# A triangular inverse built by levels: small products as 32x32 blocks on four sub-arrays, in place of 64x64 products

## The chip, the cores and the metric

The kernel runs on one core of a Trainium2 chip. The metric is the device time of one execution in microseconds. A core has a matrix engine (TensorE, PE in the tables; its weight loads are listed apart as PEld), a vector engine (DVE), a scalar engine (ACT), a third elementwise engine (POOL) and queues for transfers, which SyncE (SP) fills. Each works through its own list of instructions in order and waits for the others by semaphores. Matrix products are written to PSUM, eight banks of 512 f32 values on each of 128 partitions; everything else is held in SBUF, also 128 partitions.

## What is computed

A trunk of two layers over 528 positions of 1024 features (16 learned ones, then 512 of the input). Each layer is a half-step SwiGLU FFN, a token mixer, and another half-step FFN, with RMSNorm before and after each. The first layer's mixer is RWKV-7 time mixing, the second's is windowed attention. The change lies in the recurrence of the first mixer alone, with 16 heads of 64 features:

```python
def step(S, inp):
    r_t, w_t, k_t, v_t, a_t, b_t = inp
    sa = jnp.einsum('bhij,bhj->bhi', S, a_t)
    S = S * w_t[:, :, None, :] + sa[..., None] * b_t[:, :, None, :] + v_t[..., None] * k_t[:, :, None, :]
    return S, jnp.einsum('bhij,bhj->bhi', S, r_t)
...
_, y = lax.scan(step, jnp.zeros((B, H, N, N), f32), seq)
```

## The kernel before

The recurrence isn't run token by token. The function `core` cuts the (padded) 576 positions into NRC = 9 chunks of CH = 64 tokens. Inside a chunk each `sa` depends on the earlier ones through a strictly lower triangular 64x64 matrix, so the kernel needs the inverse of a unit triangular matrix for each head and chunk. It builds it by levels: X starts as the identity plus the entries below the diagonal within pairs of tokens, and a level l joins blocks of 2^(l-1) rows into blocks of twice that:

- `up(l, n)`: U = N_l times X, where N_l is the chunk's matrix masked to level l (levels 2 to 5; POOL makes these, L1933).
- ACT copies U from PSUM to SBUF (`copy_u`, L1783; level 6: L1786).
- `across(l, n)`: T = U times X again, in the turned form XT.
- DVE adds T to XT (`grow`, L1872) and transposes it into X by blocks of 32x32 (L1874). Level 6 only adds (L1879).

After level 5, X consists of two 32x32 blocks on the diagonal of each head's 64x64; for levels 2 to 5 all that is outside of these two blocks is zero in N_l, X, U and T. Level 6 fills the remaining corner, by `corner` (L1649 for U6, L1646 for T6), which already uses 32x32 products. Chunk 0 has no levels 5 and 6 (its first 48 positions are padding).

Layout: a pair of heads lies on the 128 partitions, one on 0 to 63 and one on 64 to 127, and there are eight pairs. Each step is done in two halves, f = 0 and 1, of four pairs. `product` (L1634) makes one matmul of 64x64 for each pair and head, so 8 for a half; operands are f32. A half of U or T lies in one PSUM bank: banks 0 and 1 hold U, 2 and 3 hold T, in the lower 256 of 512 values; `bank` gives this view.

PE's order is written out by hand in `pe`, as a software pipeline: while chunk n grows its inverse, the state products of chunk n-1 (`state_sa`, `state_s`, `state_y`), the turned operands of chunk n (`turn`, L1658: Vt, Bt, Kt) and the scores of chunk n+1 (`scores`, L1625: A, K) are put between the levels. For n at or above 1 the order is: U2 T2, SA, U3, S, T3, Y, U4, Vt Bt, A, T4, Kt, U5, K, T5, R, U6 T6. The first chunk lacks what belongs to chunk n-1 and levels 5 and 6.

Of the kernel before, what the change touches and what calls it, by code (L numbers as in the profile page):

```python
# [22 lines left out]
ALU = mybir.AluOpType  # L23
# [3 lines left out]
P = 128  # L27
# [8 lines left out]
HD = 64  # L36
# [5 lines left out]
PAIRS = HEADS // 2  # L42
# [55 lines left out]
def build(nc, xT, vecs, consts, w_gu, w_down, w_rkv, w_l1, w_g1, w_w2, w_a2, w_g2, w_out, w_q, w_k, w_v, b_v,  # L98
          w_o, rel_table, rel_hot, flip_rows, out):
    with ExitStack() as ctx:  # L100
# [15 lines left out]
        psum = ctx.enter_context(nc.psum_tensor("psum", [P, 8, 512], F32))  # L116
# [44 lines left out]
        freed = sem("banks_freed")  # L161
# [21 lines left out]
        class Plan:  # L183
# [6 lines left out]
            x = 0  # L190
# [1338 lines left out]
        def core(d_dve, c_scan, cbuf, r_end):  # L1529
# [4 lines left out]
            N = PAIRS * CH  # L1534
# [13 lines left out]
            bs = (buf(stf, 0, 2 * CH), buf(stf, 2 * N, 2 * CH))  # L1548
# [10 lines left out]
            def first(t):  # L1559
                return t[:, :, 0:CH]  # L1560
# [39 lines left out]
            def bank(n, f):  # L1600
                return psum[:, BANK[n][f], 0:N // 2].rearrange("p (q t) -> p q t", q=PAIRS // 2)

            def bank2(n, f):
                return psum[:, BANK[n][f], :].rearrange("p (q t) -> p q t", q=PAIRS // 2)

# [12 lines left out]
            def pe(e):  # L1618
# [10 lines left out]
                def product(o, f, *terms):  # L1629

                    for q in range(4):
                        for p0 in (0, HD):
                            for z, (a, b) in enumerate(terms):
                                last = e.matmul(o[p0:p0 + HD, q], a[p0:p0 + HD, 4 * f + q, 0:CH],  # L1634
                                                b[p0:p0 + HD, 4 * f + q, 0:CH],
                                                start=(z == 0), stop=(z == len(terms) - 1))
                    return last

                def corner(o, f, turned, x, xt, nt):
# [34 lines left out]
                def up(l, n):  # L1674
                    for f in range(2):
                        if l == 2:
                            after(e, i_dve, f"X{f}", n)
                        else:
                            after(e, l_dve, f"X{l - 1}_{f}", n)
                        if l < 6:  # L1680
                            after(e, i_pool, f"N{l}", n)
                            last = product(bank("U", f), f, (Nk[l], X[n % 2]))
                        else:
                            last = corner(bank("U", f), f, False, X[n % 2], XT[n % 2], first(bs[n % 2]))
                        last.then_inc(l_pe.sem, l_pe.step(f"U{l}_{f}"))

                def across(l, n):
                    for f in range(2):
                        after(e, l_act, f"U{l}_{f}", n)
                        if l == 2:  # L1690
                            after(e, l_dve, f"T6_{f}" if n > 1 else f"T4_{f}", n - 1)
                        if l < 6:
                            last = product(bank("T", f), f, (U, XT[n % 2]))
                        else:
                            last = corner(bank("T", f), f, True, X[n % 2], XT[n % 2], first(bs[n % 2]))
                        last.then_inc(l_pe.sem, l_pe.step(f"T{l}_{f}"))

                def state_r(i):
# [26 lines left out]
                        product(bank("Y", f), f, *held_state, (Vt, second(ks[i % 2])),  # L1725
                                (SA, second(bs[i % 2]))).then_inc(s_pe.sem, s_pe.step(f"Y{f}"))

                e.wait_ge(s_init, 2)
                scores_a(0)
                scores_k(0)  # L1730
                for n in range(NRC):
# [99 lines left out]
            def dve(e):  # L1831
# [32 lines left out]
                def grow(l, n):  # L1864
                    for f in range(2):
# [10 lines left out]
                        else:  # L1876
                            for p0 in (0, 64):
                                x = xt[p0:p0 + 32, :, 32:64]
                                ins = e.tensor_tensor(x, x, bank("T", f)[p0:p0 + 32, :, 32:64], ALU.add)  # L1879
                            ins.then_inc(l_dve.sem, l_dve.step(f"T{l}_{f}"))  # L1880

                def state(i):
# [9 lines left out]
                e.wait_ge(d_dve.sem, d_dve.count(f"b{KT - 1}"))  # L1892
                e.memset(ST[0][:, :, :], 0.0).then_inc(s_init, 1)
                e.memset(dec[:, :, 0:1], 1.0).then_inc(s_init, 1)
                e.wait_ge(s_init, 2)
                inverse_operands(0)
                decay_operands(0)
                masked("A", bs, 0)
# [970 lines left out]
```

## Time and profile before

| | |
|---|---|
| median of 3 runs | 2287.49 us (2283.71 to 2288.39) |
| the profiled execution | 2284.82 us |
| its span, first to last instruction | 2283.0 us |
| PE busy, share of the span | 2202.5 us, 96% |
| DVE, ACT, POOL busy | 48%, 35%, 20% |
| mean granted clock of PE | 0.975 |
| the core's stretch | 594.8 to about 818 us |

The page gives busy time by engine. The busy time of PE is a sum over modelled ends, so it can't be read as peak use. Further down the page, "the chain that ended last" goes back from the last instruction, at each step to what released it; the shares are of the span. In the rows, a line such as L1634 is a line of the kernel before. "64*64 64x64 f32" is the part of the array in use (rows*columns) and the moving operand's shape. A timeline row gives the start, the time to the end of the last record in the group, engine, line, operation, output<-inputs, the count of records, and in brackets the engine's idle time before it and what ended that. A matmul on f32 data is two records. Names are those of the SBUF areas: Nk and X, U lie in `split`, XT and one of the states in `cumsum_buf`, the masked scores in `stage`.

### The profile page before, as it was taken

To read this page: it belongs to the slowest core of one execution; us is meant where nothing else is said; L and a number is where in the kernel's file an instruction comes from. 1 tells how busy PE (TensorE), PEld (TensorE's weight loads), DVE (VectorE), ACT (ScalarE), POOL (GpSimd) and SP (SyncE) were. 2 spreads that over 40 slices of the span, in tenths; PEclk is the share of its full clock that TensorE was granted. 3 is DMA by queue.
4 is the path that set the end of the run, shared out by engine and by line. 5 is a ranking of instruction groups with operands and counts; after the bars stand their busy time and mean duration, and the time that the engine had idled before them with its cause. 6 is when DMAs were issued, how large, how long until landed. Compare 5 with 4: busy or idle time off the path is not lost.

```text
span 2283.0 us, 51042 instructions
## 1 busy us (share of the span) xinstructions
PE 2202.5 (96%) x22812; PEld 1867.3 (82%) x22812; DVE 1092.4 (48%) x1562; ACT 804.8 (35%) x1388; POOL 467.9 (20%) x595
## 2 busy tenths in 40 slices
PE   7999998999899999999999999999998999999997
PEld 6888887877699965788888888888886667888886
DVE  5433325767566555843332563333274537433323
ACT  4333313565233343533331343332142424433320
POOL 2111112420223223511110221110151204111102
PEclk9999999999999999999999999999999779999999
DMA  4323321320000012232232122232132012323311
GB/s 160 130 93 105 123 88 38 131 68 20 13 4 4 4 57 94 80 124 99 100 127 88 50 100 102 103 121 102 56 92 84 1 37 75 111 93 118 127 52 38
DMA packets 29099, 183.43 MB, mean 80 GB/s; under 512 B 3232, under 2 KB 8160, under 8 KB 9936
## 3 DMA queue, kind: packets, MB, share of 16 engines
q1 hardware_dynamic: 28032, 178.79, 22.3%
q8 instruction: 180, 2.95, 0.5%
q0 software_dynamic: 848, 1.37, 0.3%
q14 instruction: 39, 0.32, 0.0%
HBM read 174.31 MB, written 4.30 MB: 78 GB/s over the span
## 4 chain that ended last, share of the span: by engine, by line
PE 85%; DVE 10%; ACT 3%; POOL 1%; issue 1%; DMA 0%; SPq 0%; DVEq 0%; POOLq 0%; ACTq 0%
PE psum L289 67%; PE psum L1634 6%; DVE arena L355 2%; DVE arena L403 1%; PE psum L1625 1%; PE psum L381 1%; PE psum L2527 1%; PE psum L2526 1%; PE psum L2513 1%; PE psum L1658 1%; DVE arena L393 1%; DVE arena L331 1%; DVE split L264 1%; PE psum L2357 1%; DVE h L360 1%
## 5 line engine op out<-in xcount | busy, mean ns | idle before, releaser
L289 PE MATMUL psum<-x,split 128*128 128x256 f16 (+1 forms) x5568 | 638.7, 276 | 7.1 <-POOL x L422 5.5
L289 PEld LDWEIGHTS psum<-x,split 128*128 128x128 f16 x5568 | 542.9, 98 | 99.3 <-issue 15.1
L289 PE MATMUL psum<-x,split_more 128*128 128x256 f16 (+1 forms) x2496 | 287.1, 276 | 2.5 <-DVE x L2625 1.5
L289 PE MATMUL psum<-x,arena 128*128 128x256 f16 (+2 forms) x2448 | 281.1, 276 | 7.6 <-DVE arena L657 6.8
L725 POOL TENSOR_TENSOR arena<-arena 128x256 f16<-128x256 f32 (+1 forms) x176 | 120.4, 684 | 797.6 <-ACT arena L574 797.6
L289 PEld LDWEIGHTS psum<-x,split_more 128*128 128x128 f16 x2496 | 244.6, 98 | 39.6 <-issue 1.9
L289 PEld LDWEIGHTS psum<-x,arena 128*128 128x128 f16 (+1 forms) x2448 | 240.2, 98 | 43.1 <-DVE arena L264 7.3
L264 DVE SCALAR_TENSOR_TENSOR split<-stage,split 128x2048 f16<-128x2048 f32 (+1 forms) x77 | 189.9, 2467 | 157.4 <-ACT split L258 157.4
L289 PE MATMUL psum<-arena,split 128*128 128x256 f16 (+1 forms) x2304 | 261.6, 275 | 0.0
L289 PEld LDWEIGHTS psum<-arena,split 128*128 128x128 f16 x2304 | 225.4, 98 | 35.0 <-issue 2.5
L652 DVE SCALAR_TENSOR_TENSOR arena<-psum,arena 128x256 f32<-128x256 f32 (+1 forms) x176 | 75.5, 429 | 311.1 <-ACT arena L568 306.4
L568 ACT ACTIVATE arena<-psum 128x256 f32<-128x256 f32 (+1 forms) x176 | 68.3, 388 | 371.8 <-PE psum L289 371.7
L467 ACT ACTIVATE arena<-arena 128x272 f32<-128x272 f32 (+1 forms) x96 | 38.8, 419 | 364.3 <-DVE arena L454 342.4
L258 ACT ACTIVATE split<-stage 128x2048 f16<-128x2048 f32 (+1 forms) x77 | 156.2, 2028 | 26.8 <-PE psum L289 25.5
L454 DVE TENSOR_SCALAR arena<-psum 128x272 f32<-128x272 f32 (+1 forms) x80 | 33.3, 428 | 246.6 <-PE psum L289 246.6
L574 ACT ACTIVATE arena<-arena 128x256 f16<-128x256 f32 (+1 forms) x176 | 74.1, 421 | 200.7 <-DVE arena L657 200.7
L289 PE MATMUL psum<-arena,split_more 128*128 128x256 f16 (+3 forms) x1248 | 143.5, 275 | 0.3
L289 PEld LDWEIGHTS psum<-arena,split_more 128*128 128x128 f16 (+1 forms) x1248 | 121.2, 98 | 21.2 <-issue 2.6
L478 POOL TENSOR_TENSOR arena<-arena 128x272 f32<-128x272 f32 (+1 forms) x84 | 65.9, 784 | 348.3 <-ACT arena L467 344.8
L289 PE MATMUL psum<-arena 128*128 128x256 f16 (+2 forms) x1200 | 136.7, 275 | 0.0
L289 PEld LDWEIGHTS psum<-arena 128*128 128x128 f16 (+1 forms) x1200 | 117.8, 98 | 16.9 <-POOL arena L997 0.3
L264 DVE SCALAR_TENSOR_TENSOR split_more<-stage,split_more 128x2048 f16<-128x2048 f32 (+2 forms) x36 | 88.3, 2453 | 80.6 <-ACT split_more L258 80.6
(220 smaller groups left out, 2601.6 us busy)
## 6 DMA issues: line engine op xcount, KB each, us to landing
stage<-in_w_gu SPq DMA_DIRECT2D x88, 1024.0 KB, 4.9
stage<-in_w_down SPq DMA_DIRECT2D x32, 1408.0 KB, 6.1
stage<-in_w_rkv SPq DMA_DIRECT2D x12, 1024.0 KB, 5.0
stage<-in_w_out SPq DMA_DIRECT2D x4, 1024.0 KB, 4.7
stage<-in_w_q SPq DMA_DIRECT2D x4, 1024.0 KB, 4.8
stage<-in_w_o SPq DMA_DIRECT2D x4, 1024.0 KB, 5.7
h_spill<-h SPq DMA_DIRECT2D x1, 2112.0 KB, 12.0
out<-h SPq DMA_DIRECT2D x8, 256.0 KB, 2.1
```

Of the source, the lines that this page charges most:

```text
L258: act.activation(job.split[:, 0, 0:job.cols], stage[:, job.u, 0:job.cols], ACT.Copy, scale=W_SCALE).then_inc(w_hi, 1)
L264: dve.scalar_tensor_tensor(out=job.split[:, 1, 0:job.cols], in0=stage[:, job.u, 0:job.cols], scalar=W_SCALE, in1=job.split[:, 0, 0:job.col ...
L289: last = pe.matmul(o, wt(wp, k), xs(xp, k), start=(k == 0 and wp == 0 and xp == 0), stop=(k == tiles - 1 and wp == 1))
L355: dve.scalar_tensor_tensor(out=tmp[:, k % 4, 0:n], in0=mix_out[:, k, a:a + n], scalar=v("gain", T.post_gain + k), in1=rinv[:, a:a + n], op ...
L454: ins = dve.tensor_scalar(mix_out[:, m, a:a + n], bank(i, z)[:, 0:n], 1.0 / W_SCALE, None, ALU.mult)
L467: act.activation(osq[:, q % 2, 0:n], mix_out[:, m, a:a + n], ACT.Square).then_inc(out_sq, 1)
L478: pool.tensor_tensor(ssum[:, a:a + n], ssum[:, a:a + n], osq[:, q % 2, 0:n], ALU.add).then_inc(out_add, 1)
L568: e.activation(gate_s[:, no % 2, 0:n], bank(i)[:, 0:n], ACT.Sigmoid, scale=1.0 / W_SCALE).then_inc(gate_act, 1)
L574: e.activation(hid[s][:, 0, m, 0:n], hid32[:, no % 2, 0:n], ACT.Copy).then_inc(hid_hi, 1)
L652: e.scalar_tensor_tensor(out=gate_x[:, no % 2, 0:n], in0=bank(i)[:, 0:n], scalar=1.0 / W_SCALE ** 2, in1=gate_s[:, no % 2, 0:n], op0=ALU.m ...
L725: e.tensor_tensor(hid[s][:, 1, m, 0:n], hid32[:, no % 2, 0:n], hid[s][:, 0, m, 0:n], ALU.subtract).then_inc(hid_lo, 1)
L1634: last = e.matmul(o[p0:p0 + HD, q], a[p0:p0 + HD, 4 * f + q, 0:CH], b[p0:p0 + HD, 4 * f + q, 0:CH], start=(z == 0), stop=(z == len(terms) ...
```

## The change

Three things:

- A new function `blocks` takes the place of `product` in `up` and `across` for levels below 6. For each of the four pairs it issues four matmuls of 32x32, at partitions 0, 32, 64 and 96 (the two diagonal blocks of each of two heads), so 16 for a half in place of 8. Each works on its own 32 rows and 32 columns of the array. What lies outside the blocks in U's and T's banks isn't written any more.
- DVE adds whole banks of T to XT, so the rest of T's banks has to be zero: a memset before the first chunk sets the lower halves of banks 2 and 3 to zero, once the banks of the step before are free. The turned corner of level 6 would write there; it now goes to the upper halves of the same banks (`upper`).
- The semaphore on which PE and DVE wait before the core (`s_init`) counts the memset too: 3 in place of 2.

```diff
@@ -1600,6 +1600,9 @@
             def bank(n, f):
                 return psum[:, BANK[n][f], 0:N // 2].rearrange("p (q t) -> p q t", q=PAIRS // 2)
 
+            def upper(n, f):
+                return psum[:, BANK[n][f], N // 2:N].rearrange("p (q t) -> p q t", q=PAIRS // 2)
+
             def bank2(n, f):
                 return psum[:, BANK[n][f], :].rearrange("p (q t) -> p q t", q=PAIRS // 2)
 
@@ -1634,6 +1637,14 @@
                                 last = e.matmul(o[p0:p0 + HD, q], a[p0:p0 + HD, 4 * f + q, 0:CH],
                                                 b[p0:p0 + HD, 4 * f + q, 0:CH],
                                                 start=(z == 0), stop=(z == len(terms) - 1))
+                    return last
+
+                def blocks(o, f, a, b):
+
+                    for q in range(4):
+                        for p0 in range(0, P, 32):
+                            r, t = slice(p0, p0 + 32), slice(p0 % HD, p0 % HD + 32)
+                            last = e.matmul(o[r, q, t], a[r, 4 * f + q, t], b[r, 4 * f + q, t], start=True, stop=True)
                     return last
 
                 def corner(o, f, turned, x, xt, nt):
@@ -1679,7 +1690,7 @@
                             after(e, l_dve, f"X{l - 1}_{f}", n)
                         if l < 6:
                             after(e, i_pool, f"N{l}", n)
-                            last = product(bank("U", f), f, (Nk[l], X[n % 2]))
+                            last = blocks(bank("U", f), f, Nk[l], X[n % 2])
                         else:
                             last = corner(bank("U", f), f, False, X[n % 2], XT[n % 2], first(bs[n % 2]))
                         last.then_inc(l_pe.sem, l_pe.step(f"U{l}_{f}"))
@@ -1690,9 +1701,9 @@
                         if l == 2:
                             after(e, l_dve, f"T6_{f}" if n > 1 else f"T4_{f}", n - 1)
                         if l < 6:
-                            last = product(bank("T", f), f, (U, XT[n % 2]))
+                            last = blocks(bank("T", f), f, U, XT[n % 2])
                         else:
-                            last = corner(bank("T", f), f, True, X[n % 2], XT[n % 2], first(bs[n % 2]))
+                            last = corner(upper("T", f), f, True, X[n % 2], XT[n % 2], first(bs[n % 2]))
                         last.then_inc(l_pe.sem, l_pe.step(f"T{l}_{f}"))
 
                 def state_r(i):
@@ -1725,7 +1736,7 @@
                         product(bank("Y", f), f, *held_state, (Vt, second(ks[i % 2])),
                                 (SA, second(bs[i % 2]))).then_inc(s_pe.sem, s_pe.step(f"Y{f}"))
 
-                e.wait_ge(s_init, 2)
+                e.wait_ge(s_init, 3)
                 scores_a(0)
                 scores_k(0)
                 for n in range(NRC):
@@ -1876,7 +1887,7 @@
                         else:
                             for p0 in (0, 64):
                                 x = xt[p0:p0 + 32, :, 32:64]
-                                ins = e.tensor_tensor(x, x, bank("T", f)[p0:p0 + 32, :, 32:64], ALU.add)
+                                ins = e.tensor_tensor(x, x, upper("T", f)[p0:p0 + 32, :, 32:64], ALU.add)
                             ins.then_inc(l_dve.sem, l_dve.step(f"T{l}_{f}"))
 
                 def state(i):
@@ -1892,7 +1903,9 @@
                 e.wait_ge(d_dve.sem, d_dve.count(f"b{KT - 1}"))
                 e.memset(ST[0][:, :, :], 0.0).then_inc(s_init, 1)
                 e.memset(dec[:, :, 0:1], 1.0).then_inc(s_init, 1)
-                e.wait_ge(s_init, 2)
+                e.wait_ge(freed, r_end + 1)
+                e.memset(psum[:, BANK["T"][0]:BANK["T"][1] + 1, 0:N // 2], 0.0).then_inc(s_init, 1)
+                e.wait_ge(s_init, 3)
                 inverse_operands(0)
                 decay_operands(0)
                 masked("A", bs, 0)
```

The order of the steps is the same on each engine; what changes is the form of the instructions. On PE, the start of a chunk from the second on: U2 (`split`), T2 (`cumsum_buf,split`), SA (`split,cumsum_buf`), U3, and the first of S. Before:

```order
L1634 MATMUL psum<-split 64x64 [waits start_pool,start_dve]
L1634 MATMUL psum<-split 64x64 x7
...
L1634 MATMUL psum<-cumsum_buf,split 64x64 [waits levels_dve,levels_act]
L1634 MATMUL psum<-cumsum_buf,split 64x64 x7
...
L1634 MATMUL psum<-split,cumsum_buf 64x64 [waits levels_dve,state_act]
L1634 MATMUL psum<-split,cumsum_buf 64x64 x7
...
L1634 MATMUL psum<-split 64x64 [waits start_pool,levels_dve]
L1634 MATMUL psum<-split 64x64 x7
...
L1634 MATMUL psum<-stage 64x64 [waits state_act,levels_act]
```

And now, at the same place:

```order
L1647 MATMUL psum<-split 32x32 [waits start_pool,start_dve]
L1647 MATMUL psum<-split 32x32 x15
...
L1647 MATMUL psum<-cumsum_buf,split 32x32 [waits levels_dve,levels_act]
L1647 MATMUL psum<-cumsum_buf,split 32x32 x15
...
L1637 MATMUL psum<-split,cumsum_buf 64x64 [waits levels_dve,state_act]
L1637 MATMUL psum<-split,cumsum_buf 64x64 x7
...
L1647 MATMUL psum<-split 32x32 [waits start_pool,levels_dve]
L1647 MATMUL psum<-split 32x32 x15
...
L1637 MATMUL psum<-stage 64x64 [waits state_act,levels_act]
```

Where a half stood as 8 matmuls of 64x64 there are 16 of 32x32, with the same waits; between them the state's products stay 64x64. On DVE, the start of the core, now:

```order
L1904 MEMSET split 128x512 [waits kk_dve]
L1905 MEMSET x 128x8
L1907 MEMSET psum 128x2x256 [waits banks_freed]
L1850 TENSOR_TENSOR x<-arena,x 128x512 [waits operands_act,core_constants]
```

The third row is new; the others are those of before.

## Rows read from the trace of the kernel before

**Rows 1.** Page: the chain that ended last, by engine and by line.
```profile
PE 85%; DVE 10%; ACT 3%; POOL 1%; issue 1%; DMA 0%; SPq 0%; DVEq 0%; POOLq 0%; ACTq 0%
PE psum L289 67%; PE psum L1634 6%; DVE arena L355 2%; DVE arena L403 1%; PE psum L1625 1%; PE psum L381 1%; PE psum L2527 1%; PE psum L2526 1%; PE psum L2513 1%; PE psum L1658 1%; DVE arena L393 1%; DVE arena L331 1%; DVE split L264 1%; PE psum L2357 1%; DVE h L360 1%
```

**Rows 2.** Two lines of the core: durations ns (min/median/max), first and last start.
```profile
L1625 PE MATMUL psum<-x x320: 269/269/469, 594.8 to 787.3; 64*64 64x128 f32 x160
...
L1634 PE MATMUL psum<-stage,split x288: 218/218/218, 630.5 to 817.7; 64*64 64x64 f32 x144
```

**Rows 3.** Busy time by stretch, PE: one period, then 640 to 820.
```profile
core 0: us, PE busy (x), PEclk, DMA share, GB/s
666.00:690.30 24.30, 23.68 (x742) 1.00 0.02 4
...
640.00:820.00 180.00, 174.38 (x5421) 1.00 0.02 5
```

**Rows 4.** Waits of PE, 640 to 790 us: in total, times, longest.
```profile
PE psum L1646 <- ACT split L1786: 2.5, 6, 0.4
```

**Rows 5.** Timeline of PE (start, duration, records): U2, SA, U3; then U5; last the next U2.
```profile
695.30 1.15 PE L1634 MATMUL psum<-split 64*64 64x64 f32 x32
...
697.44 1.10 PE L1634 MATMUL psum<-split,cumsum_buf 64*64 64x64 f32 x32
698.38 1.24 PE L1634 MATMUL psum<-split 64*64 64x64 f32 x32
...
711.62 1.36 PE L1634 MATMUL psum<-split 64*64 64x64 f32 x31
...
719.57 0.33 PE L1634 MATMUL psum<-split 64*64 64x64 f32 x4
```

**Rows 6.** Timeline: U6 and T6; last, durations (ns) of U6's line.
```profile
693.23 0.69 PE L1649 MATMUL psum<-split,stage 32*32 32x32 f32 x32
...
694.35 1.02 PE L1646 MATMUL psum<-cumsum_buf,split 32*32 32x32 f32 x32 [0.42 <-ACT split L1786]
...
L1649 PE MATMUL psum<-split,stage x256: 191/191/212, 644.7 to 811.7; 32*32 32x32 f32 x128
```

**Rows 7.** Timeline of PE: what overlaps 693.245:693.25, then 693.288:693.292.
```profile
693.23 0.22 PE L1649 MATMUL psum<-split,stage 32*32 32x32 f32 x2
...
693.23 0.24 PE L1649 MATMUL psum<-split,stage 32*32 32x32 f32 x3
```

**Rows 8.** Timeline of PE: start of the two-term product R.
```profile
691.22 0.33 PE L1634 MATMUL psum<-cumsum_buf,x 64*64 64x64 f32 x4
691.34 0.33 PE L1634 MATMUL psum<-stage 64*64 64x64 f32 x4
```

**Rows 9.** Timeline of PE: what overlaps 693.235:693.24, then 695.18:695.35.
```profile
693.03 0.28 PE L1634 MATMUL psum<-stage 64*64 64x64 f32 x3
...
695.01 0.36 PE L1646 MATMUL psum<-cumsum_buf,split 32*32 32x32 f32 x12
695.30 0.27 PE L1634 MATMUL psum<-split 64*64 64x64 f32 x2
```

**Rows 10.** Timeline of ACT, then of DVE, at level 2.
```profile
696.02 0.85 ACT L1783 ACTIVATE split<-psum 128x256 f32<-128x256 f32 x2 [1.15 <-PE psum L1634]
...
697.19 0.42 DVE L1872 TENSOR_TENSOR cumsum_buf<-cumsum_buf,psum 128x256 f32<-128x256 f32 x1 [1.17 <-PE psum L1634]
...
698.43 0.45 DVE L1874 STREAM_TRANSPOSE split<-cumsum_buf 128x256 f32<-128x256 f32 x1
```

**Rows 11.** Timeline of DVE at the start of the core.
```profile
590.86 0.48 DVE L1893 MEMSET split<- 128x512 f32 x1
...
592.12 2.50 DVE L1839 TENSOR_TENSOR x<-arena,x 128x512 f32<-128x512 f32 x4 [0.76 <-ACT x L1776]
```

**Rows 12.** By stretch: PE, PEld, DVE, ACT, POOL busy; granted clock; first chunk.
```profile
609.00:612.00 3.00, 0.96 (x22) 0.74 (x22) 2.93 (x7) 0.22 (x1) 0.00 (x0) 0.92 0.00 0
...
611.80:614.90 3.10, 3.10 (x58) 3.10 (x60) 1.21 (x3) 0.97 (x3) 0.00 (x0) 0.50 0.02 5
```

## The prediction

> **What bounds the kernel now.** I began with the page: TensorE (PE) holds 85% of the chain that ended last, and the core of the time mixing, which is the only place the change touches, has two lines in that chain, L1634 with 6% and L1625 with 1% [rows 1]. The core runs from 594.8 to about 818 us [rows 2], nine chunks of 64 tokens. The next view is the table by stretch, cut at one period, 24.3 us: over one such stretch PE shows 23.68 us busy at a granted clock of 1.00, so at 2.4 GHz [rows 3]. Busy time of PE contains the modelled tails of pipelined products, so I then looked at the list of waits: over six chunks PE has only 2.5 us of recorded waiting, all of it at the corner products of level 6 [rows 4]. So a chunk lasts as long as PE needs to start its records, plus some short waits. What the reader should take from this: here the *spacing of the starts* is the price of a product, not the 218 ns that one record lasts.
>
> That spacing stands in the timeline of one chunk. One matmul of the program is two records in the trace (f32 in two passes), so one half (f) of a level product, 8 matmuls of 64x64, is 16 records. Two halves without a wait in them run from 697.44 to 698.38: 0.47 us a half [rows 5]. One such chunk begins with U2 at 695.30, the next at 719.57, 24.27 us later [rows 5]. Two sub-arrays (rows 0 and 64) share the 16 records, so each sub-array takes a new one every 58 ns. The corner products, already 32x32, take 0.69 us for 32 records, less the 0.19 us of the last one: 0.50 us for 32 starts, 0.25 us a half [rows 6]. Narrow windows show how: by 693.25 two have started, one on either sub-array, and a third only by 693.29 [rows 7]; then it is a pair every 32 ns (0.50 us over 16 pairs).
>
> **Term A, the products themselves.** The new function `blocks` puts a half of a level product into 16 matmuls of 32x32, 32 records, on four sub-arrays. Each sub-array gets 8 records, exactly what each of the two gets in a half of a corner. If the four run beside one another, a half costs what a corner's half costs: 8 x 32 ns = 0.26 us in place of 0.47. If only two run at a time, as in every row that there is, it is 16 x 32 ns = 0.51 us, more than before. These are the two ends, and no trace row shows four at once. I take 0.26, for this reason: within a pair the starts lie under 15 ns apart (both after 693.23, both before 693.245), while a sub-array repeats after 32 ns [rows 6, 7], so the limit is the sub-array and not the place that hands records out; for four of them it has to hand out one record every 8 ns, which the pairs allow but don't show. Nor does the program's order hold sub-arrays up: in a two-term product the program gives both terms of sub-array 0 before those of sub-array 64, four records, but the trace shows four records of the first operand and then four of the second: the other sub-array was started past the ones waiting [rows 8]. A chunk has 16 such halves (levels 2 to 5, `up` and `across`, two halves): 16 x 0.21 = **-3.3 us a chunk**. At 0.51 it is +0.7.
>
> The Trainium skill speaks against this change: TensorEngine Tiling, Gotcha 1, says that different row tiles cannot access the same PSUM bank at the same time, and all four row groups of `blocks` write one bank. Taken strictly it would make 32 x 32 ns = 1.0 us of a half. This case's rows already contradict the strict form: in a corner, rows 0 and 64 write one bank and start under 15 ns apart. By that rule, if it bound only beyond two, the sum would be that of the first rival below; by the skill's TensorE: Matmul & The Clock Gate, Part 3, which states four row tiles at 3.07 times the rate of one, a half would be, as an estimate, 1.02 / 3.07 = 0.33 us, and the result near the third rival.
>
> **Term B, changes of tile size.** Before, a chunk leaves the 64x64 tiling once, for U6 and T6. Now it is {U6 T6 U2 T2}, U3, T3, U4, T4, U5, T5, seven stretches in 32x32 with 64x64 work (SA, S, Y, Vt/Bt/A, Kt, K, R) between them: six round trips more. Price from the rows: the last three 64x64 records start from 693.03 on and end at 693.31, so the last started at 693.09, and the corner at 693.23: 0.15 us where 0.06 is normal, +0.09 [rows 9]. Back: 695.37 less 0.19 is 695.18, and U2 starts at 695.30: 0.12 where 0.03 is normal, +0.09 [rows 9]. Then the pipeline refills: U2 takes 1.15 us where SA, without a stop ahead of it, takes 1.10 [rows 5], and a corner some 0.02. Neither start had a semaphore that was late. Together 0.25 us: 6 x 0.25 = **+1.5 us a chunk**. Ends: 6 x 0.18 if the refill hides, and 6 x 0.35 if four sub-arrays drain worse than two.
>
> **Term C, waits that come out.** The helpers (ACT copies, DVE adds and transposes) stay the same in number and size, and PE reaches them sooner.
> - T2 behind U2: the copy of half 0 starts at 696.02, 0.26 after that half's last record, takes 0.38, and the semaphore 0.05 [rows 10]: T2 can start 0.70 us after the last record of half 0 (0.67 with 32x32 records, whose tail is 0.03 shorter). Half 1 covers 0.47 of it now and 0.26 then: the wait grows from 0.23 (U2's last start at 696.23, T2's first at 696.46, which is SA's start less 0.98 [rows 5]) to 0.41; and half 1 of T2 then catches up with the second copy: some 0.1 more. +0.3.
> - U3's second half needs the second transpose. Add, transpose, add, transpose run from 697.19 to 698.88 [rows 10], with 0.24 ahead and 0.05 behind it some 1.98 us after T2's first half. PE's cover is T2's rest 0.36, SA 0.98 with its refill, two changes 0.2 and half of U3 0.26: 1.8. The wait is about 0.2 and was 0.14 (1.24 us of U3 against 1.10): +0.1.
> - U5's second half waits 0.26 us now: its 32 records take 1.36, not 1.10 [rows 5]. DVE does the second mask of A (0.69) before T4's add, so its chain is tied to the end of A and hardly moves, while PE's cover shrinks by T4 and half of U5 (0.6 us) and gains three half changes (0.3): +0.3.
> - U6, T6 are unchanged; T3 and U4 have the 1.9 us of S or the 2.8 us of Y ahead of them, and T5 the scores K; no wait there.
> Sum **+0.7 us a chunk** (0.3 to 1.2).
>
> **The rest.** DVE gets a memset of 512 elements of PSUM at the start. It stands where DVE is idle 0.76 us for the exponential on ACT, from 591.37 to 592.12 [rows 11]; the memset of the same size in SBUF takes 0.48 us, so it is hidden; bounds 0 and +0.2 us. The level 6 turned corner only uses another half of its bank: nothing.
>
> A chunk: -3.3 + 1.5 + 0.7 = -1.1 us, for the eight chunks after the first -8.8. The first chunk has no level 5, and the helpers' chain sets its pace; that chain holds a half of U and of T in each of three levels, 6 x 0.21 less about two changes of size: -0.8. Together **-9.6 us**. The profiled execution took 2284.82 us (span 2283.0), so 2275.2; it lies 2.7 us below the median of the runs, 2287.49, and against that median the same gain gives 2277.9. I predict 2278. The rest of the kernel starts earlier and does the same.
>
> **Rivals.** (A difference under 0.2%, 4.6 us, can't be told from none here.)
> 1. *Slower: two sub-arrays at a time.* Place: inside every half of `blocks`, by the shared bank or because the two passes of a matmul are handed out in order. Price: +0.05 x 16 = +0.7, changes +1.5, and PE, slower than now, finds the helpers ready: its short waits (0.6 us a chunk without level 6) all but go. Some +1.5 a chunk, +12 in all: 2299. It decides from 0.35 us a half on, where A (-1.9), B and the rest of C cancel. For it: no row has a start rate above two in 32 ns. Against: the pairs and the order of the two-term product [rows 7, 8]. Chance 0.14.
> 2. *The clock.* With more stops between small tiles, the chip may grant half clock in the stretch U6 to T2, where waits add up to 1.3 us. In the first chunk the grant was 0.50 from 611.8 to 614.9, after PE had been idle for 2.0 of the 3 us before [rows 12]; such a stretch costs half of itself, 1.6 us. Once a chunk: +13 less 9.6, so 2291. Against: from 640 to 820 us the grant stayed at 1.00, with a whole microsecond of stops at every level 6 [rows 3, 4, 6]. Chance 0.07.
> 3. *A draw.* A half takes 0.32 to 0.38 us because four sub-arrays start staggered, or a change costs 0.4 us: A is -1.6 to -2.4 or B +2.4, and the result is -4 to 0: 2285. Chance 0.15.
> 4. My forecast, -5 to -13 us: 0.62. The remaining 0.02 is anything else.
>
> The likeliest case reaches from 2272 to 2284 by itself. With the lower end of B and C (1.1 + 0.3) and 0.255 a half, the gain would be 1.9 a chunk and 16 in all: 2271. The other end is the first rival, 2298. Chances: faster 0.64 (the forecast and a little of the third), same 0.15, slower 0.21.
>
> **What would show it.** Term A: the two halves of U3 or T3 in 32x32 form take near 0.7 us as one group (0.50 + 0.19), not 1.2. Four records of `blocks` must begin within 32 ns, over a whole half. Term B: gaps of 0.15 and 0.12 us at seven places in a chunk. Term C: T2 begins about 0.4 us after U2's last start. Period of a chunk: 23.1 to 23.2 us in place of 24.27; granted clock 1.00 from the second chunk on. I am wrong in A if the period is above 25 us; wrong in B or C if a group of `blocks` takes 0.7 us and the period is still 24; wrong on the clock if stretches under 1.00 appear there. The memset is wrong if the first DVE operand of the core starts after 592.3.

## The result, and the profile after

The changed kernel takes 2325.03 us (median of 4, 2322.38 to 2331.53) beside 2287.05 us for the kernel before (median of 4, 2283.71 to 2288.39). The ratio is 1.0179, with a 95% interval of 1.0161 to 1.0197. It is slower by 38 us, where 9.6 us of gain were forecast, and it lies outside the range. The profiled execution took 2322.38 us (span 2320.6, before 2283.0), so the 37.6 us between the two spans are what the traces have to explain.

The page of the changed kernel: first its busy times, then the granted clock in 40 slices, and from the part on DMA queues the one row that turned out to matter.

```profile
span 2320.6 us, 55523 instructions
...
PE 2213.1 (95%) x25052; PEld 1866.5 (80%) x25052; DVE 1093.0 (47%) x1563; ACT 803.4 (35%) x1388; POOL 467.3 (20%) x595
...
PEclk9999999999898899999999999999999779999999
...
q8 instruction: 198, 3.24, 0.6%
```

The slices of the core (from about 593 to 850 us) stand at 8 and 9. The row of q8 in the page of before:

```profile
q8 instruction: 180, 2.95, 0.5%
```

Its kind is "instruction", and by the count it carries the program of PE: 198 packets of 256 instructions are 50,688, and the trace has 50,632 of PE (25,052 matmuls, as many weight loads, 528 of its sequencer); before it was 46,080 beside 46,152. Next, PE by stretch: three chunks, and the answer to the window of 180 us in [rows 3].

```profile
core 0: us, PE busy (x), PEclk, DMA share, GB/s
646.40:674.80 28.40, 23.58 (x997) 1.00 0.02 4
674.80:703.20 28.40, 23.93 (x993) 1.00 0.02 5
...
731.30:761.30 30.00, 27.17 (x995) 0.83 0.02 4
...
640.00:820.00 180.00, 157.59 (x6167) 0.91 0.02 5
```

From U6 to U6 the chunks last 28.38, 28.46, 28.04, 29.98, 29.91, 29.23 and 26.72 us, where they lasted 24.27 (the last, with no scores in it, 20.88). In the first two the clock is full and PE is *not* busier than before (23.6 and 23.9 us against 23.68 [rows 3]); it is idle for 4.5 to 4.8 us. The list of waits says where. These are all the rows of over half a microsecond, 640 to 820 us (in total, times, longest), in place of the single row of [rows 4]:

```profile
engine line waited for: us in total, times, longest us
PE psum L1647 <- issue: 8.7, 14, 1.7
PE psum L1637 <- issue: 3.8, 5, 1.5
PE psum L1657 <- ACT split L1797: 2.6, 6, 0.5
PE psum L1669 <- issue: 2.0, 3, 1.0
PE psum L1660 <- issue: 1.2, 2, 0.8
PE psum L1647 <- ACT split L1794: 1.2, 6, 0.2
PE psum L1647 <- DVE split L1885: 0.9, 4, 0.2
```

L1647 is `blocks`, L1637 `product`, L1657 and L1660 the corners T6 and U6. The wait for ACT at T6 is the old one. The new ones are of a kind that no row before had: "issue", a wait for nothing that the profile shows, and it falls on many lines of PE, not on the changed one alone. The timeline shows one of them from close by (start, duration, records): T2, SA, U3.

```profile
678.13 0.78 PE L1647 MATMUL psum<-cumsum_buf,split 32*32 32x32 f32 x64 [0.18 <-ACT split L1794]
678.84 0.79 PE L1637 MATMUL psum<-split,cumsum_buf 64*64 64x64 f32 x19
681.10 0.62 PE L1637 MATMUL psum<-split,cumsum_buf 64*64 64x64 f32 x13 [1.48 <-issue]
681.65 0.75 PE L1647 MATMUL psum<-split 32*32 32x32 f32 x64
```

The two groups of `blocks` hold both halves and take 0.78 and 0.75 us, near the 0.7 of Term A. But SA, which the change does not touch, stops for 1.48 us after 19 of its 32 records, in the middle of a product whose semaphores it had already waited for.

**What the stops are.** Every matmul record has a weight load beside it, and both are instructions of PE. Counted in the traces, PE has 1491 instructions in a chunk before and 2003 after (16 halves, 32 more in each). A packet of q8 has 16,384 bytes for 256 instructions, so 64 bytes each. From 640 to 840 us there are 45 places where PE's next matmul starts over 0.2 us after the last one without a late semaphore. Eight of them are of 0.23 to 0.24 us, at changes of tile size, seven of them at half clock. The other 37 hold 27.8 us, counted from start to start (the rows of waits begin only where the last record's modelled 0.22 us ends, and show less), and *every distance from one of them to the next is a multiple of 256 instructions* (256, 512, 768 or 1024, give or take one). I call such a stretch of 256 instructions a batch.

The packets stand in a fixed relation to the batches, one to each. In the 19 batches that begin and end with a stop, the transfer begins 1.06 to 1.74 us (median 1.22) after PE has entered the batch and takes 0.88 to 1.34 us, and PE goes on 1.20 to 1.51 us after it has landed. For the stop above: PE enters the batch at 677.34, the packet starts at 678.90 and lands at 679.83, and SA goes on at 681.10. No second packet of q8 was under way beside one. Such a batch lasts 3.28 to 4.36 us. All batches that end in a stop last 2.90 to 4.36 us, 3.62 in the mean. The shortest is one whose packet had started early, 0.70 us into the batch (PE enters it at 648.34); PE is through its 256 instructions in 1.6 us and stands for the other 1.3. 2003 / 256 x 3.62 = 28.3 us, and the measured period is 28.4. This is the same trace counted in two ways, so it shows only that the stops fill up the period; whether the time follows the count is for the experiments.

The Trainium skill, Runtime: NRT & Kernel Launch, section Instruction fetch mechanics, says that the sequencer fetches its instructions in blocks of 256 by a DMA queue of its own while the current block executes, and that this is mostly hidden. The distances in this trace agree on the 256. On "hidden" the measurement decides: here it is not hidden.

Before the change there was one packet for every 256 instructions too, and nobody waited: 1491 / 256 is 5.8 packets in 24.27 us, 4.2 us each. But where 64x64 products stand close, 256 instructions took only 3.67 to 3.74 us, which is within the range of the stopped batches. The kernel was already close to the limit there, and no row of waits shows that, because the wait was still zero.

The second difference is the clock. From the third of these chunks on there are stretches at half clock, one of them here (PE busy, granted clock):

```profile
707.20:713.90 6.70, 6.18 (x157) 0.50 0.01 4
```

The grant falls at 707.1, 734.4, 765.1, 795.8, 826.6 and 850.5 us, 3.1 to 6.2 us after a U6 began. Behind the first five of these U6 come T6, U2 and T2, now all of them 32x32 work; behind the last, in the last chunk, there is no U2 and no T2. The first two U6 of the table (646.4 and 674.8 us) are followed by no fall. Before, the grant stayed at 1.00 from 615 us to the end of the core.

Last the memset (DVE at the core's start), beside [rows 11]:

```profile
589.18 0.48 DVE L1904 MEMSET split<- 128x512 f32 x1
589.62 0.07 DVE L1905 MEMSET x<- 128x8 f32 x1
589.79 0.48 DVE L1907 MEMSET psum<- 128x512 f32 x1
590.45 0.69 DVE L1850 TENSOR_TENSOR x<-arena,x 128x512 f32<-128x512 f32 x1 [0.17 <-ACT x L1787]
```

It takes 0.48 us, and DVE's idle time for the exponential shrinks from 0.76 to 0.17 us. From the first memset to the first operand it is 1.27 us, before 1.26: hidden, as forecast.

### The profile page after: what moved, and what is told of

The parts are those of the page before. It is cut to its first block, busy times and chain, and to the rows that moved or that the text cites. A ratio compares the mean times of both kernels' runs of the same rounds, so it can differ in the third digit from the quotient of the medians.

```text
span 2320.6 us, 55523 instructions
## 1 busy us (share of the span) xinstructions
PE 2213.1 (95%) x25052; PEld 1866.5 (80%) x25052; DVE 1093.0 (47%) x1563; ACT 803.4 (35%) x1388; POOL 467.3 (20%) x595
## 4 chain that ended last, share of the span: by engine, by line
PE 84%; DVE 10%; ACT 3%; issue 2%; POOL 1%; DMA 0%; SPq 0%; DVEq 0%; POOLq 0%; ACTq 0%
PE psum L289 66%; PE psum L1637 4%; PE psum L1647 2%; DVE arena L355 2%; DVE arena L403 2%; PE psum L1628 1%; PE psum L2540 1%; PE psum L381 1%; PE psum L2539 1%; PE psum L1669 1%; PE psum L2526 1%; DVE split L264 1%; DVE arena L393 1%; DVE arena L331 1%; PE psum L2370 1%
## 5 line engine op out<-in xcount | busy, mean ns | idle before, releaser
L289 PEld LDWEIGHTS psum<-x,arena 128*128 128x128 f16 (+1 forms) x2448 | 240.6, 98 | 42.4 <-DVE arena L264 7.3
```

The lines of the kernel that those rows point to most:

```text
L289: last = pe.matmul(o, wt(wp, k), xs(xp, k), start=(k == 0 and wp == 0 and xp == 0), stop=(k == tiles - 1 and wp == 1))
```

## The experiments

Three theories could explain the stops and the time. *Supply*: the engine waits for its own instructions, so the time follows their number, above all their number in a dense stretch. *Tiles*: changes of tile size cost more than the traces say. *Arrays*: four sub-arrays in one bank hold one another up. Eleven kernels tell them apart. The period is that from U6 to U6. All times are medians, and each ratio is to the kernel before on the same chip (medians 2285.2, 2287.6, 2283.6 and 2284.9 us).

**1. Half of the pairs (`half_blocks`).** As many instructions as before, 1491, in the new tiles and on four sub-arrays.

```diff
 def blocks(o, f, a, b):
-    for q in range(4):
+    for q in range(2):
```

> Each level product in 32x32 form is done for two of the four pairs only (this leaves out half of the levels' work), so a half is 16 records per pass count as before the change, with all changes of tile size kept. Instruction supply theory (the trace of the changed kernel shows PE standing still in the middle of products, every 256 records, while a 16 KB instruction packet is under way; a packet comes every 3.6 us, and a chunk has 2003 records where it had 1491): back at 1491 records the supply allows 21.1 us a chunk, PE needs some 21.7, so 12 to 21 us faster than before, about 2270. Tile change theory (the twelve added changes between 64x64 and 32x32 cost 0.45 us each, not 0.12): all changes are still there, a chunk near 27 us, 20 us or more slower than before, about 2309.

Measured: 2275.52 us, ratio 0.9959 (0.9944 to 0.9974). Periods 22.4 to 23.2 us; waits for "issue" 0.6 us from 640 to 820, beside some 16 in the changed kernel. The stops go with the number of instructions, not with the tiles, and not with four sub-arrays in one bank, which this kernel has too. The gain, 9 us, is smaller than the 12 to 21 expected: the helpers now set part of the pace, and PE waits 3.3 us for DVE's second transposes (L1885) and 2.2 for ACT at T2, 640 to 790 us; the granted clock also fell three times, for 3.4 us each.

**2. Only T in blocks (`across_blocks`, 1747), 3. levels 2 and 3 (`levels_2_3`, 1747), 4. level 2 (`level_2`, 1619).** Full work. Both calls are edited alike, with `l <= 3` or `l == 2`; 2. takes the `product` back for U alone.

```diff
-    last = blocks(bank("U", f), f, Nk[l], X[n % 2])
+    last = blocks(...) if l <= 3 else product(bank("U", f), f, (Nk[l], X[n % 2]))
```

> 32x32 blocks in across (T) alone, up (U) as before: 8 of 16 halves, 1747 records a chunk, four added round trips between tile sizes. Supply theory: 1747/256 x 3.63 = 24.8 us a chunk, +0.5 on 24.27, so 4 to 10 us slower than before, about 2293, and no different from the kernel with levels 2 and 3 alone, which has the same count. Tile change theory: four of six round trips at 0.9 us, a chunk near 27 us, 20 to 25 us slower, about 2310.

> 32x32 blocks in levels 2 and 3 alone, both up and across: again 8 of 16 halves and 1747 records a chunk, but two added round trips between tile sizes. Supply theory: as with across alone, 24.8 us a chunk, 4 to 10 us slower than before, about 2293. Tile change theory: two of six round trips, near 25.2 us a chunk, about 8 us slower; the two kernels must differ by some 15 us.

> 32x32 blocks in level 2 alone, which lies right behind level 6 of the chunk before and so adds no change of tile size: 4 of 16 halves, 1619 records a chunk. Supply theory: the supply allows 22.95 us, PE needs 23.7, so PE bounds again: 2 to 5 us faster than before, about 2283, if no single stretch outruns the supply. Tile change theory: the same, 4 us faster. This one is not to tell them apart, but to see whether a part of the change beats the kernel before.

Measured: `across_blocks` 2296.74 (1.0050, 1.0031 to 1.0070), periods 25.4 to 26.8. `levels_2_3` 2308.71 (1.0105, 1.0087 to 1.0122), periods 26.0 to 27.8. `level_2` 2297.93 (1.0063, 1.0041 to 1.0085), periods 24.7 to 26.6. The theory of dear tiles wanted the first to be the slower of the first two, by 15 us; it is the faster by 12. But the supply theory's numbers are missed as well: the first is 11 us slower where 4 to 10 were expected, the second 24 where 4 to 10 were, and the third 14 us slower where a gain was expected, since 1619 instructions need only 6.3 packets, 23 us at the 3.63 us each that the estimates used. Two things were missing from that average. The packets don't even out over a chunk: where the 32x32 products stand together, in U2, T2 and what follows, the stop comes at once (`level_2`):

```profile
698.60 0.54 PE L1647 MATMUL psum<-cumsum_buf,split 32*32 32x32 f32 x22 [1.32 <-issue]
```

And the clock falls: in `level_2` at 647.3, 698.5 and 821.4 us, in `levels_2_3` at 683.4, 707.3 and 734.6, while `across_blocks`, which has only T2 there, keeps 1.00 throughout.

**5. T4 and T5 in blocks (`t4_t5_blocks`, 1619).** As many instructions as `level_2`, but beside sparse work (the scores are 64x128 products, 269 ns a record [rows 2]). U keeps the product, T has `if l > 3`.

> 32x32 blocks in T4 and T5 alone: 4 of 16 halves, 1619 records a chunk as in the kernel with level 2 alone (measured 12.7 us slower), but these two stand behind the 64x128 score products, where records are half as dense, and add two round trips between tile sizes. Supply theory: what counts is that no 256 records in a row run in under 3.6 us, so here there are hardly any stops: within 3 us of before, about 2284. If the count of a chunk alone decided, it would be some 12 us slower, as level 2 is.

Measured: 2286.82 us (10 runs), ratio 1.0005 (0.9996 to 1.0015); period 24.17, twice 24.6 to 24.7; 1.3 us of "issue" from 640 to 820 against 6.6 in `level_2`. Same count, 11 us apart (13 by the two ratios): it is how close the instructions stand over the length of a packet (and the clock) that costs, not the count of a chunk.

**6. The changes of tile alone (`tiles_only`, 1515).** The kernel before, with one 32x32 matmul ahead of six halves, into a bank that the product then overwrites: six stretches, twelve changes of size.

```diff
+if l > 2 and f == 0:
+    tiny(bank("U", f))        # 32x32, eye by eye
 last = product(bank("U", f), f, (Nk[l], X[n % 2]))
```

> The kernel before, with one 32x32 product (4 records, overwritten at once) ahead of each of the six stretches U3, T3, U4, T4, U5, T5: it adds the twelve changes of tile size a chunk and only 24 records. Supply theory: the changes cost what term B says, 1.5 us a chunk, so 10 to 14 us slower than before, about 2297. Tile change theory: they carry most of the loss, 4 to 5 us a chunk, 35 us or more slower, about 2322.

Measured: 2298.99 us, ratio 1.0057 (1.0042 to 1.0073); period 25.84 in six of seven chunks (the last is shorter, as everywhere), clock 1.00 in these, no wait for "issue". By stretch, one period of PE:

```profile
648.70:674.50 25.80, 25.23 (x749) 1.00 0.01 4
```

25.84 - 24.27 = 1.57 us a chunk for six round trips. That is Term B (1.5), and the theory of dear tiles falls.

**7. The moving side cut in two (`mv_split`, 2003), 8. the same with one piece (`mv_half`, 1491).** The kernel before in 64x64 tiles; each level matmul becomes two of 32 moving columns, or just the first. `mv_half` has the memset of the changed kernel as well. The pair was meant to add instructions without any change of tile.

```diff
+for z in parts:                     # (0, 32), or (0,)
+    last = e.matmul(o[p0:p0+HD, q, z:z+32], a[p0:p0+HD, 4*f+q, 0:CH],
+                    b[p0:p0+HD, 4*f+q, z:z+32], start=True, stop=True)
```

> The kernel before, all level products in the 64x64 tile, but each matmul cut into two over columns 0 to 31 and 32 to 63 of the moving operand: 2003 records a chunk as in the changed kernel, no 32x32 tile and no added change of tile size, the arithmetic the same. Supply theory: at least 28.4 us a chunk (2003/256 x 3.63), 35 us or more slower than before, about 2322, with stops every 256 records in the middle of products. If instead the loads of 64 weights set the pace (58 ns a record), PE alone needs 31.7 us a chunk, 65 us slower, and there are no such stops. Tile change theory: no slower than the load of weights makes it; with records at 32 ns, no loss at all, about 2285.

> The kernel before, all level products in the 64x64 tile, with the moving operand cut to columns 0 to 31 (this leaves out half of each level product): 1491 records a chunk as before, no change of tile size added. Supply theory: a packet of 256 records can't take less than some 3.6 us, and the kernel before is at 3.7 already in stretches of 64x64 products, so the gain is capped: a chunk of 21.1 us at best, more likely 22 to 23, 8 to 18 us faster, about 2273, with stops every 256 records. If the loads of weights set the pace, no gain: 2285. Without a limit of supply, PE would need 24.3 - 3.3 + 0.7 = 21.6 us.

Measured: `mv_half` 2289.39 us (10 runs), ratio 1.0015 (1.0000 to 1.0029), period 24.22, in one chunk 25.66, where the granted clock fell to half for 3.4 us (at 697.5): half of the moving columns bring nothing, each sub-array still takes a record every 58 ns. So `mv_split`, with twice the records, needs 31.7 us a chunk at that pace and can't reach the limit of the supply: no stop at 256 instructions in it. It does not test what it was made for. It took 2382.4 us (1.0421, 1.0384 to 1.0459) with periods of 37.3 us (one of 35.7), longer than 31.7, with a fall of the clock in every chunk (PE, two stretches):

```profile
640.00:820.00 180.00, 177.21 (x4861) 0.83 0.02 4
...
663.00:676.40 13.40, 13.40 (x256) 0.50 0.01 2
```

PE is busy for all of the 13.40 us and stands at half clock all the same. Ahead of the fall, at 662.87, it had stopped only at T6, for ACT, as in the kernel before (0.42 us; it was busy for 3.31 of the 3.87 us from 659.00 on).

**9. Two sub-arrays (`two_arrays`, 1491).** The same tiles, halves, changes and helpers as the changed kernel, 8 x 32 ns a half as in Term A, but only the blocks at partitions 0 and 64, so 512 instructions fewer.

```diff
-for p0 in range(0, P, 32):
+for p0 in range(0, P, 64):
```

> The changed kernel with the blocks at partitions 0 and 64 only (this leaves out the blocks of rows 32 to 63 of each head): the same 32x32 groups, the same changes of tile size, each half on two sub-arrays with 8 records each, so each half should last the same 0.26 us, but with 1491 records a chunk in place of 2003. The two other sub-arrays only add records, no time, if the four run beside one another. Supply theory: this is the kernel that the prediction thought it was timing; few stops in the middle of products, a chunk of 23.0 to 23.6 us, 5 to 10 us faster than before, about 2280. If anything else in the changed kernel costs the time (changes of tile size, waits for ACT and DVE, 32-row products as such), it is here too, and this kernel stays 20 us or more slower than before, about 2310.

Measured: 2282.61 us (10 runs), ratio 0.9993 (0.9981 to 1.0006), so no difference from before can be told; periods 22.97, 24.16, 25.58, 23.56, 23.00, 25.57, 20.29, no wait for "issue". First a chunk at full clock, then a stretch after U6 at half:

```profile
643.40:666.35 22.95, 21.79 (x737) 1.00 0.02 4
...
693.90:700.50 6.60, 6.60 (x136) 0.50 0.01 4
```

At full clock the period is 23.0 us in two chunks, which is the forecast of 23.1 to 23.2, and 23.56 in a third. Most of the expected gain is missing where the clock falls, at 669.9, 693.8 and 765.5 us, 2.8 to 3.6 us behind U6; these chunks last 1.2, 2.6 and 2.6 us more than 23.0.

**10. Levels 3 to 5, two sub-arrays (`levels_345_two`, 1491), 11. the same on four (`levels_345`, 1875).** Level 2 goes back to `product` (`if l > 2`), which takes the 32x32 work behind U6 and T6 away, the suspected reason of the clock. The second then does the full work, with 384 instructions more a chunk.

> As the kernel with two arrays (blocks at partitions 0 and 64 only, which leaves out half of the levels' work), but level 2 is again 64x64 products, so that the stretch of 32x32 work from U6 to T2 ends with T6. 1491 records a chunk. In the kernel with two arrays the granted clock fell to half some 3 us after U6 in three of seven chunks, and chunks took 23.0 us at full clock but up to 25.6 with a fall. Clock theory (the falls come from the sparse stretch made of level 6 and a 32x32 level 2 behind it): no falls from 640 us on, every chunk at 24.27 - 12 x 0.21 + 1.5 + 0.4 = 23.6 us, 4 to 7 us faster than before, about 2282. If the falls come from 32x32 work as such, wherever it stands: they stay, at some chunks, and the kernel is within 2 us of before.

> The changed kernel with level 2 again as 64x64 products, blocks on four sub-arrays in levels 3 to 5 (the full work): 12 of 16 halves, 1875 records a chunk. Supply theory: at least 1875/256 x 3.63 = 26.6 us a chunk, so 18 to 27 us slower than before, about 2309, with stops every 256 records; against the kernel of the same form on two arrays the only difference is 384 more records, which by term A take no time of their own. If supply doesn't matter there: about 2282, like that one. Clock theory: few or no falls of the granted clock from 640 us on, except those that the stops themselves bring.

Measured: `levels_345_two` 2279.56 us (10 runs), ratio 0.9985 (0.9975 to 0.9996), periods 23.64, 23.64, 23.81, 24.06, 23.64, 23.65, 20.08 where 23.6 was expected; by the ratio it is 3 us faster than before, a little under the 4 to 7 expected. `levels_345` 2317.16 us, 1.0143 (1.0128 to 1.0158), periods 26.4 to 29.1, with 37 stops from 640 to 840 us, 26.8 us in all, again at multiples of 256 instructions. It is 33 us slower than before, where 18 to 27 were expected: its batches that end in a stop last 3.76 us in the mean, more than the 3.63 of the estimate. One chunk of the first, two of the second:

```profile
645.54:669.18 23.64, 22.73 (x739) 1.00 0.02 4
```

```profile
648.60:675.90 27.30, 24.32 (x933) 1.00 0.02 4
675.90:704.30 28.40, 24.41 (x931) 1.00 0.02 4
```

The clock is 1.00 in both from 640 to 840 us, so it is not what separates them. The same two places of a chunk, U3 and T3, in the first kernel (two sub-arrays):

```profile
650.78 0.90 PE L1647 MATMUL psum<-split 32*32 32x32 f32 x32
...
653.66 0.69 PE L1647 MATMUL psum<-cumsum_buf,split 32*32 32x32 f32 x32
```

and in the second (four):

```profile
653.87 0.91 PE L1647 MATMUL psum<-split 32*32 32x32 f32 x64
...
656.77 0.43 PE L1647 MATMUL psum<-cumsum_buf,split 32*32 32x32 f32 x27
657.92 0.52 PE L1647 MATMUL psum<-cumsum_buf,split 32*32 32x32 f32 x37 [0.72 <-issue]
```

In U3 four sub-arrays take 64 records in the time in which two take 32, 0.91 against 0.90 us. Both hold a short wait for the transpose ahead of the second half; without one, 64 records take 0.75 us (U3 of the changed kernel, 681.65 above) and 32 take 0.69 (T3 here). T3 on four sub-arrays is cut by a stop of 0.72. That pair is the whole case: the array does the extra work for almost nothing, and the engine doesn't get the instructions for it in time.

## Why the prediction was wrong

**Term A: nearly right in its price, wrong in its condition.** Groups of both halves, 64 records, take 0.74 to 0.78 us without a wait at full clock; less the 0.19 of the last record that is 0.28 us a half, where 0.26 was forecast (-3.0 us a chunk in place of -3.3). Narrow windows around 681.66 us in the changed kernel show four starts within 20 ns (what overlaps 681.66 to 681.668, then 681.67 to 681.68). The next four begin 33 ns behind the fourth, so I read them as one on each sub-array:

```profile
681.65 0.23 PE L1647 MATMUL psum<-split 32*32 32x32 f32 x3
```

```profile
681.65 0.23 PE L1647 MATMUL psum<-split 32*32 32x32 f32 x4
```

What failed is the step from "so the limit is the sub-array and not the place that hands records out" to a price of 8 x 32 ns for every half. I had looked at that place for one group of starts and took it to be free on that ground; it can hand out four in 20 ns from what it holds. What has to *bring* the instructions had no term in the sum, and 512 more of them a chunk were costed at nothing; no rival named it either, so the cause lay in the 0.02 of "anything else". The edit from `two_arrays` to the changed kernel adds those instructions alone: 2282.61 and 2325.03 us, **42.4 us** (42.5 by the two ratios), though with them the clock falls more often, six times in place of three. `levels_345_two` and `levels_345` are at full clock both: 37.6 us for 384. What four sub-arrays cost beside two, where no stop falls into them, is 0.06 us for each of eight steps, 4 us in all.

**Term B: right.** 1.57 us a chunk by `tiles_only` against 1.5. In the changed kernel's records the gaps are 0.15 us from 64x64 to 32x32 (0.20 behind the scores) and 0.12 back, as from [rows 9].

**Term C: right as far as it shows.** T2 begins 0.37 to 0.41 us after U2's last start (forecast 0.41). A, B and C together are tested by the chunks at full clock: 23.0 us, once 23.56, in `two_arrays` (forecast 23.1 to 23.2) and, without level 2, 23.64. In the list of waits of `two_arrays`, 640 to 790 us, ACT at T2 holds 1.3 us and the second transposes (L1885) 1.9 us, 0.5 us a chunk together: the waits that Term C named.

**The rest: right.** The memset is hidden. The start of the core had moved 1.7 us earlier in the profiled execution (593.1 against 594.8), which is no part of the loss.

**Rival 1, two sub-arrays at a time: wrong**, though its sign came true. The four go beside one another in one bank. The Trainium skill's rule (TensorEngine Tiling, Gotcha 1), that different row tiles can't access one PSUM bank at the same time, is not borne out by this trace in either form: one at a time would make 1.0 us of a half and two at a time 0.51, and 0.28 was measured.

**Rival 2, the clock: real, for a small part, and its reason stays open.** It was costed at 1.6 us a fall, for stops in U6 to T2. The falls do come behind a U6, mostly by 3 to 6 us. The stops alone don't bring them: the wait ahead of T6 stands in the kernel before as well, `across_blocks` and `levels_345` have the issue stops besides, and in neither does the grant fall from 640 to 840 us. Most falls come where small products follow level 6, 32x32 ones or those of 32 moving columns (`mv_split`, `mv_half`). But that isn't a rule either: `levels_345` falls at 842.0, 0.8 us behind its last U6, `tiles_only` and `t4_t5_blocks` fall 3 us behind theirs, `levels_2_3` once 8.6 us behind one, the changed kernel at 850.5 with no level 2 behind, `mv_half` in one chunk only. Its price is 2282.6 less the forecast of 2278, some 4.6 us, taken from `two_arrays`; that it is the same in the changed kernel is an assumption. There the chunks with a fall last 28.0 to 30.0 us where those without last 28.4, 3.5 us more over four of them.

**The sum.** 2278 (A, B, C hold) + 4.6 (clock) + 42.4 (supply) = 2325. It closes by the way the two differences are formed. A check that doesn't use these medians goes by the periods, 28.4 measured at full clock and 23.1 forecast: (28.4 - 23.1) x 8 chunks = 42.

**What the profile before would have told.** Two rows that I did not weigh: the q8 row of the DMA part, 180 packets, and the 742 records of a chunk in [rows 3], which with their loads make nearly all of the 1491 instructions. Beside the packets in that trace, of which one goes with every 256 instructions, and these last only 3.7 us in the dense stretches, a change that puts 34% more instructions into the same time had to be priced against the supply, at least as a rival. The limit itself can't be read there, as nothing waits.

**What stays open.** Why PE goes on only 1.2 to 1.5 us after a packet has landed, and why no second packet is fetched ahead, no run here tells, nor what makes the clock fall. How much of the loss of `level_2` is clock and how much supply was not separated. Extra 32x32 records put *into* the 64x64 tiling were not tried. None of the versions with the full work beats the kernel before; `t4_t5_blocks` ties with it.

## What to carry to other kernels

Treat the instructions of TensorE as a resource with a rate: here 256 of them (a matmul in f32 is four) took 3.6 us in the mean wherever they had to be waited for (2.9 to 4.4), and a kernel can be close to that limit with no wait to show for it. Cutting a product into smaller ones that use more of the array pays only where the instructions around them are few in that time, so put it beside long-running products and count per 256, not per loop. When waits for "issue" appear on lines that the change didn't touch, count the instructions between them before looking for a dependency.

## What the runs showed of the hardware

- The supply of instructions to PE in the changed kernel: one packet of 16,384 bytes at a time on q8 for each 256 instructions, 1.06 to 1.74 us until it starts, 0.88 to 1.34 (median 0.96) to transfer, 1.20 to 1.51 until PE goes on.
- Four sub-arrays on the diagonal take a record each every 32 ns while they write one PSUM bank (64 records in 0.75 us, 32 records on two sub-arrays in 0.69); one round trip between 64x64 and 32x32 tiles costs 1.57 / 6 = 0.26 us, with the small product that makes it (`tiles_only`).
- In 64x64 tiles and f32 a sub-array takes a record every 58 ns even with 32 moving columns (`mv_half`), so its moving columns don't set that pace. With 32x32 weights and 32 columns it is 32 ns.
- The granted clock stayed at 0.50 under matmuls that never paused, for 13.4 us of most periods of 37.3 in `mv_split`. In several kernels with small products behind level 6 it fell some 3 to 6 us behind U6, once 8.6; `across_blocks`, with 23 stops from 640 to 800 us, kept 1.00.
